# Moving the buffer of turned inputs by 32 bytes in a two-block transformer kernel

## Time and profile before

| | us |
|---|---|
| median of 3 runs | 1422.8 (1422.3 to 1424.75) |
| the profiled execution, device time | 1423.93 |
| its span, first to last instruction | 1422.1 |
| TensorE's mean granted clock | 0.997 of full |
| PE busy | 1409.4 |
| DVE busy / ACT busy | 925.0 / 741.1 |

### The profile page before, as it was taken

How to read it: one execution, slowest core, us unless ns; L and a number is a source line. 1 busy time by engine, 2 the same in 40 slices (tenths; PEclk the granted TensorE clock), 3 DMA queues, 4 the chain that set the end, 5 groups by cost and what they waited for, 6 DMA issues and landing times.

```text
span 1422.1 us, 23069 instructions
## 1 busy us (share of the span) xinstructions
PE 1409.4 (99%) x8950; PEld 1276.1 (90%) x8950; DVE 925.0 (65%) x1340; ACT 741.1 (52%) x1007; POOL 62.9 (4%) x89
## 2 busy tenths in 40 slices
PE   9999999999999999999999999999999999999998
PEld 8999999999988888899888888888889999888886
DVE  5555788675666656768666666666657578666656
ACT  6556673344355444558654545544545258554454
POOL 2000010010010000010120000100000000200000
PEclk9999999999999999999999999999999999999999
DMA  8444441255545555462375555755555400455552
GB/s 322 169 159 136 162 148 60 90 193 182 191 143 200 203 180 201 155 201 76 125 268 203 194 189 178 241 202 179 179 200 183 148 31 2 175 210 192 188 196 89
DMA packets 34630, 239.69 MB, mean 169 GB/s; under 512 B 3898, under 2 KB 4042, under 8 KB 6656
## 3 DMA queue, kind: packets, MB, share of 16 engines
q1 hardware_dynamic: 32832, 231.52, 46.6%
q0 software_dynamic: 1440, 6.67, 1.5%
q10 hardware_dynamic: 288, 0.52, 0.1%
HBM read 237.10 MB, written 1.08 MB: 167 GB/s over the span
## 4 chain that ended last, share of the span: by engine, by line
PE 95%; DVE 2%; ACT 1%; issue 1%; DMA 0%; SPq 0%; POOL 0%; POOLq 0%; ACTq 0%; DVEq 0%
PE ps L715 22%; PE ps L685 16%; PE ps L687 16%; PE ps L686 16%; PE ps L723 11%; PE ps L942 3%; PE ps L965 2%; PE ps L952 1%; PE ps L1228 1%; PE ps L2729 1%; PE ps L2737 1%; PE ps L624 1%; PE ps L2741 1%; PE ps L2904 1%; PE ps L806 1%
## 5 line engine op out<-in xcount | busy, mean ns | idle before, releaser
L392 DVE TENSOR_TENSOR low<-raw,high 128x2048 fp32r<-128x2048 f32 (+1 forms) x195 | 442.2, 2269 | 210.1 <-ACT high L386 207.8
L386 ACT ACTIVATE high<-raw 128x2048 fp32r<-128x2048 f32 (+2 forms) x198 | 374.0, 1891 | 44.1 <-PE ps L687 40.8
L715 PE MATMUL ps<-nt,high 128*128 128x512 f32 x1344 | 320.0, 390 | 0.0
L715 PEld LDWEIGHTS ps<-nt,high 128*128 128x128 f32 x1344 | 249.3, 188 | 50.6 <-issue 0.9
L685 PE MATMUL ps<-nt,high 128*128 128x256 f32 x656 | 186.9, 285 | 0.0
L686 PE MATMUL ps<-nt,high 128*128 128x256 f32 x656 | 185.6, 283 | 0.0
L687 PE MATMUL ps<-nt,low 128*128 128x256 f32 x656 | 185.6, 283 | 0.0
L723 PEld LDWEIGHTS ps<-nt,low 128*128 128x128 f32 x1344 | 167.1, 192 | 3.4
L723 PE MATMUL ps<-nt,low 128*128 128x256 f32 x1344 | 168.1, 283 | 0.0
L686 PEld LDWEIGHTS ps<-nt,high 128*128 128x128 f32 x656 | 125.9, 192 | 0.1
L685 PEld LDWEIGHTS ps<-nt,high 128*128 128x128 f32 x656 | 125.8, 192 | 0.1
(11 more groups left out here) (401 smaller groups left out, 2192.0 us busy)
## 6 DMA issues: line engine op xcount, KB each, us to landing
raw<-in_stream SPq DMA_DIRECT2D x216, 1024.0 KB, 4.9
late<-in_w POOLq DMA_DIRECT2D x1, 2048.0 KB, 9.7
scr<-bias_by_distance POOLq DMA_DIRECT2D x1, 2048.0 KB, 12.6
scr<-in_mem SPq DMA_DIRECT2D x2, 512.0 KB, 4.7
raw<-in_stream SPq DMA_DIRECT2D x4, 256.0 KB, 6.9
x<-in_x SPq DMA_DIRECT2D x1, 1024.0 KB, 12.5
con<-in_con SPq DMA_DIRECT2D x1, 592.0 KB, 12.8
row<-in_row SPq DMA_DIRECT2D x1, 592.0 KB, 14.1
```

The costliest lines, as they stand in the source:

```text
L386: nc.scalar.activation(high[t % SLOTS][:, 0:n], raw[t % SLOTS][:, 0:n], ACT.Copy).then_inc(w_high, 1)
L392: nc.vector.tensor_tensor(low[t % SLOTS][:, 0:n], raw[t % SLOTS][:, 0:n], high[t % SLOTS][:, 0:n].bitcast(F32), ALU.subtract).then_inc(w_l ...
L715: last = nc.tensor.matmul(r3(bank, 2), w[:, k, P * j:P * j + P], nt[:, :, k, :], start=first and k == 0, stop=not first and k == KC - 1, s ...
```

## The change

Two allocations of 8 floats (32 bytes in each partition) are added, one ahead of `nt` and one behind it. Nothing else is edited, and no instruction is added, removed or moved on any engine.

```diff
         xs = sb("xs", [P, TT, D])
+        sb("half_line_ahead", [P, 8])
         nt = sb("nt", [P, 2, KC, S], F32R)
+        sb("half_line_behind", [P, 8])
         nth, ntl = nt[:, 0], nt[:, 1]
```

## The result

The changed kernel takes **1430.47 us** (1430.24 to 1432.39, 4 runs) beside 1422.83 of the kernel before in the same comparison: ratio **1.0054**, 95% interval [1.0042, 1.0066], slower by 7.6 us. The forecast was 1425, range 1413 to 1431. Two executions of the kernel before in the later sets of runs, 1536 and 1732 us at a mean granted clock of 0.85 and 0.75, enter no ratio in this document.

What follows compares the result with a forecast made beforehand. PE bounds the kernel through the distances between matmul starts; -7.6 + 7.0 + 1.3 + 1.4 + 0.2 = +2.3 us takes the median from 1422.8 to 1425.1, forecast 1425, range 1413 to 1431.

Steps and rivals of the forecast that it cites:

- rival D: Wide products also pay a full line's time for the half lines in their middle, +16.5 us: 1434.6; chance 0.13.
- The sign +2.3: Whole kernel: the predicted terms sum to +2.3 us, slightly slower.
- What bounds the kernel: PE, busy 99% of the span; the time is the sum of the distances between matmul starts.
- (1) Narrow, -7.6 us: 3472 matmuls with 256 moving columns of `nt` each get 2.2 ns shorter: -7.6 us.
- Rival C: The change does nothing; the cheap `yth` rows come from the weights' chunk step, not the half line: 1422.8; chance 0.12.
- (2) Wide, +7.0 us: 1408 products with 512 moving columns of `nt` in two runs stay unsettled, 5.0 ns dearer each: +7.0 us.
- Rivals A and B: Wide products gain as narrow ones do (1413.7, chance 0.20), or stay at 227.5 ns (1416.8, chance 0.13).
- the forecast's own case: Only `nt` half a line off: narrow products faster, wide ones unsettled, +2.3 us; chance 0.42.
- (3) Down products, +1.3 us: Six down products behind the unsettled wide ones cost 5.0 ns more each, at 44 down tiles: +1.3 us.
- (4) nt stationary, +1.6 us: Products with `nt` stationary get dearer: 288 of 512 columns +1.4 us, 96 of 256 columns +0.2.
- (5) Writes, 0: Writing `nt` off a line takes ScalarE no longer than on it: 0.0 us.

Runs made afterwards that it cites:

- f2_nt32_rest256: Against the kernel before, `nt` alone moved by 32 bytes and the buffers behind it by 256: 1424.29 us, ratio 1.0007.
- g1_tail64: Against the kernel before, the last five buffers (yth, ytl, hth, htl, late) moved by 64 bytes, `nt` left in place: 1431.09 us, ratio 1.006.

## Why the prediction was right, and where it was not

The time fell inside the range, and that was luck. The forecast's own range was 1420 to 1426.3; the range reached up to 1431 only for rival D, a cost in the middle of each wide product, which no run bears out. The slowdown came from products that the sum left unchanged or nearly so. The sign +2.3 was no strong claim either: the prediction gave "same" 0.35 and "slower" 0.31. The period of a feed-forward chunk, which the prediction named to tell the cases apart, misled as well: it is 16.80 us, the figure given for D, and the down products made it so. The single groups did tell them apart: 3.73 us for 32 narrow products and 3.73 to 3.74 for 16 wide ones, beside 3.76 and 3.72 forecast.

**What bounds the kernel**: right. PE sets the time; every kernel here moved with the distances between matmul starts. (In the earlier trace rows the 0.54 of the DMA engines is a share of the time and not us.)

**(1) Narrow, -7.6 us**: measured -9.7 in the changed kernel and -8.2 in `f2_nt32_rest256`. The direction was read from `yth`, and it held; in the changed kernel 116.7 in the feed-forward chunks is the price of the earlier trace rows, 117.8 in the stretch of gates shown is that of the earlier trace rows. I took the latter for all. Rival C, that the step between weight chunks made `yth` cheap, falls: `nt` has the other step and gained as much.

**(2) Wide, +7.0 us**: measured +7.6, 233.4 ns where I had 232.5. The choice between "same operand, 256 columns" and "same length, other operand" was right: an offset of 32 bytes is cheap at 256 columns and dear at 512. The reason given for it, a stream that finds no steady pattern, doesn't hold: it finds another one. Rivals A and B fall, and D, since no group of wide products here cost 11.7 ns more. `f2_nt32_rest256` is the forecast's own case. Over its trace the terms are -8.2, +8.0, +1.0 and +1.1, together +1.8 by the unrounded terms, where the prediction had +2.3; in medians it is 0.9 us slower than the kernel before, within what the runs can tell from nothing.

**(3) Down products, +1.3 us**: this is the step that failed, measured +6.2. I gave them only the unsettled start behind the wide ones. That term is there, 1.0 us over the trace of `f2_nt32_rest256`, but in the changed kernel `hth` and `htl` themselves had moved by 64 against the weights. The sentence behind it was "Every buffer but `nt` keeps its place in the line, so the only term is how the operands of `nt` are read and written half a line off." It took 64 bytes for the unit because the change speaks of it, and no row showed that unit: all I had were buffers that agreed modulo 256 and a pair, `yth` and `ytl`, that was 32 off. The starts of `nt`, `high0` and `low0` (106624, 41088 and 65664) differ by multiples of 256, and that would have been a reason to price a shift of 64 from both sides, with the 6.6 ns of the earlier trace rows times 960 as its upper bound, 6.3 us.

**(4) nt stationary, +1.6 us**: measured +1.0. The 256-column ones gained slightly, 0.1 us in all. The same failed step left out `nt_m` and `nt_y`, +1.8.

**(5) Writes, 0**: right; DVE and ACT are busy for 925.3 and 741.2 us, beside 925.0 and 741.1.

The formula N/2.4 + 2.5 ns that the prediction quotes from the Trainium skill, page "TensorE: Matmul & The Clock Gate", section "Back-to-back issue gap", is given there for a single matmul by itself, so it was no forecast for this stream, in which each matmul has its own weight load. The conclusion that a shift by 32 or 64 bytes does nothing was drawn from two statements of the Trainium skill: the two independent read ports of "TensorE: Matmul & The Clock Gate", section "Part 2: What happens when you issue a matmul", and the 16-byte cachelines of "SBUF — State Buffer", section "Specifications (TRN2)". The runs refute the conclusion: `g1_tail64` moved the last buffers by 64 and lost 8.4 us. They do not show which of the two statements, if either, fails.

## What to carry to other kernels

A pad that is put in for one buffer moves all that lie behind it: write down the start of every stationary and moving operand before and after, and keep the others whole with a second pad, here to a multiple of 256 bytes. In a kernel bound by matmuls whose weights change each time, read the distance between starts and not the duration, and look at how long a stream takes to settle; the relative address of the two operands is then a free parameter worth 0.9% here, best found by trying a few offsets. Price a neighbour's shift like the edit itself until a row shows that it is neutral.

## What the hardware showed that I had not expected

- The spacing of a matmul stream depends on the distance between stationary and moving operand modulo 256 bytes: in the feed-forward chunks 256 columns cost 113.4 to 120.0 ns, 512 columns 226.7 to 234.4, at a granted clock of 1.00 (2.4 GHz). Moving everything by 64 changed nothing, moving one side by 64 or 128 did, and moving it by 256 did not.
- Of the offsets tried, agreement is best for 512 columns and not for 256, where an offset of 64 was 6.3 ns cheaper for each narrow product (3.63 us for 32 where agreement took 3.83).
- In the profiled executions of six of the thirteen kernels, TensorE's clock fell to half behind a row of 20 one-column products (L2839); in the other seven, with the same row, it didn't. In the kernel before, the stage view (us, then busy us and count of PE, PEld, DVE, ACT and POOL, granted clock, DMA share, GB/s) has a mean clock of 0.69 over 5 us:

```profile
620.00:625.00 5.00, 5.00 (x33) 5.00 (x33) 3.39 (x6) 0.34 (x1) 1.30 (x2) 0.69 0.57 197
```

The timeline before, inside it:

```profile
622.32 0.41 PE L685 MATMUL ps<-yth,high 128*128 128x256 f32 x1
...
624.24 0.41 PE L685 MATMUL ps<-yth,high 128*128 128x256 f32 x1
```

Nine distances in 1.92 us are 213.3 ns each, which is 256 columns at 1.2 GHz and nothing beyond: at half clock the cost beyond the columns is gone, on operands that are 32 bytes off. The 17 products from 621.70 us on take 3.60 us, where 117.9 ns each would make 2.00: 1.6 us lost. The changed kernel's profiled execution has a clock of 1.00 there, so the gap between these two single executions is smaller by about as much than that between like ones.
